# Stationary tiles of the 512-column products placed 16 words behind their streams modulo 128 (32 in the second feed-forward part) in place of 48

## The reference

```
def peer_ffn(xn, w_pq, sub_keys1, sub_keys2, expert_down, expert_up):
    def block(xb):
        qh = (xb @ w_pq).reshape(T, P_HEADS, 2, P_KEY_DIM).astype(jnp.float32)
        ...
        top_s, pos = lax.top_k(cand_s, P_TOPK)
        eidx = jnp.take_along_axis(cand_i, pos, axis=-1)
        g = jax.nn.softmax(top_s, axis=-1)
        u = expert_down[eidx]
        a = jax.nn.gelu(jnp.einsum('thkd,td->thk', u, xb), approximate=False)
        coef = (g * a.astype(jnp.float32)).astype(xb.dtype)
        return jnp.einsum('thk,thkd->td', coef, expert_up[eidx])

def conv_ffn(hn, w_up, conv_w, conv_b, w_down):
    u, v = jnp.split(hn @ w_up, 2, axis=-1)
    ...
    return (jax.nn.silu(uc) * v) @ w_down

def second_block(x, ...):
    h = x
    for layer in range(DEPTH_2):
        ...
        h = h + mix.astype(h.dtype)
        hn = rms_norm(h, ffn_norm_g[layer])
        h = h + conv_ffn(hn, ffn_w_up[layer], ffn_conv_w[layer], ffn_conv_b[layer], ffn_w_down[layer]).astype(h.dtype)
    return h
```

## Time and profile before

| what | value |
|---|---|
| runs, median (lowest to highest) | 1668.53 us (1667.17 to 1670.89) |
| span of the profiled execution | 1670.5 us |
| PE busy | 1652.9 us, 99% |
| PE's weight loads busy | 1542.5 us, 92% |
| DVE busy | 1237.3 us, 74% |
| ACT busy | 935.2 us, 56% |
| POOL busy | 242.8 us, 15% |
| DMA, mean over the span | 194 GB/s |

### The profile page before, as it was taken

How to read it: one execution, slowest core, us unless ns; L and a number is a source line. 1 busy time by engine, 2 the same in 40 slices (tenths; PEclk the granted TensorE clock), 3 DMA queues, 4 the chain that set the end, 5 groups by cost and what they waited for, 6 DMA issues and landing times.

```text
span 1670.5 us, 30280 instructions
## 1 busy us (share of the span) xinstructions
PE 1652.9 (99%) x12006; PEld 1542.5 (92%) x12006; DVE 1237.3 (74%) x1896; ACT 935.2 (56%) x1139; POOL 242.8 (15%) x333
## 2 busy tenths in 40 slices
PE   8999999999999999999999999999999999999999
PEld 8999999999999999988888888999999888899987
DVE  6875467999998666667676676887888565769974
ACT  7885565555546555545555454786545357565542
POOL 0000000004667676211010110000000000100000
PEclk9999999999999999999999999999999999999999
DMA  7445344776555555777777776533555544345553
GB/s 304 152 152 180 120 159 157 231 233 213 189 178 191 190 189 191 270 240 238 245 235 239 241 238 222 221 133 139 184 185 195 180 174 152 124 156 203 200 188 115
DMA packets 73804, 323.40 MB, mean 194 GB/s; under 512 B 8663, under 2 KB 9047, under 8 KB 55744
## 3 DMA queue, kind: packets, MB, share of 16 engines
q1 hardware_dynamic: 58736, 285.18, 50.1%
q0 software_dynamic: 5568, 19.38, 3.7%
q10 hardware_dynamic: 9360, 16.92, 2.7%
HBM read 303.62 MB, written 17.83 MB: 192 GB/s over the span
## 4 chain that ended last, share of the span: by engine, by line
PE 83%; DVE 12%; ACT 4%; issue 1%; DMA 0%; SPq 0%; ACTq 0%; DVEq 0%
PE bank L605 14%; PE bank L606 13%; PE bank L607 13%; PE bank L986 7%; PE bank L985 7%; PE bank L987 7%; PE bank L938 5%; PE bank L942 5%; PE bank L941 5%; DVE lo_u L2299 3%; PE bank L950 2%; DVE wlo L1914 2%; DVE oh L2310 1%; ACT whi L1350 1%; DVE pos L2196 1%
## 5 line engine op out<-in xcount | busy, mean ns | idle before, releaser
L1586 ACT ACTIVATE hi_u<-raw_u 128x1024 fp32r<-128x1024 f32 x256 | 271.8, 1062 | 279.6 <-PE bank L985 165.2
L1914 DVE TENSOR_TENSOR wlo<-raw,whi 128x2048 fp32r<-128x2048 f32 (+1 forms) x141 | 314.7, 2232 | 105.6 <-PE bank L605 83.3
L1350 ACT ACTIVATE whi<-raw 128x2048 fp32r<-128x2048 f32 x137 | 263.1, 1920 | 77.6 <-PE bank L605 74.7
L938 PE MATMUL bank<-xh,hi_u 128*128 128x256 f32 x1024 | 291.9, 285 | 1.5 <-DVE lo_u L2299 1.2
L2299 DVE TENSOR_TENSOR lo_u<-raw_u,hi_u 128x1024 fp32r<-128x1024 f32 x192 | 237.9, 1239 | 70.4 <-PE bank L938 62.4
L941 PE MATMUL bank<-xl,hi_u 128*128 128x256 f32 x1024 | 285.4, 279 | 0.0
L942 PE MATMUL bank<-xh,lo_u 128*128 128x256 f32 x1024 | 285.3, 279 | 0.0
L605 PE MATMUL bank<-nh,whi 128*128 128x256 f32 x904 | 253.4, 280 | 0.5 <-DVE wlo L1914 0.4
L607 PE MATMUL bank<-nh,wlo 128*128 128x256 f32 x904 | 251.9, 279 | 0.0
L606 PE MATMUL bank<-nl,whi 128*128 128x256 f32 x904 | 251.9, 279 | 0.0
L519 POOL TENSOR_SCALAR oh<-kept,sel_T 128x128 f32<-128x128 f32 x256 | 199.9, 797 | 249.3 <-ACT sel_T L1636 166.4
(11 more groups left out here) (417 smaller groups left out, 3358.7 us busy)
## 6 DMA issues: line engine op xcount, KB each, us to landing
raw<-in_weights SPq DMA_DIRECT2D x138, 1024.0 KB, 4.8
raw_u<-in_experts SPq DMA_DIRECT2D x256, 512.0 KB, 4.2
aside<-a_out ACTq DMA_DIRECT2D x64, 256.0 KB, 3.6
a_in<-aside POOLq DMA_DIRECT2D x64, 256.0 KB, 3.7
const<-in_const SPq DMA_DIRECT2D x1, 1409.0 KB, 9.0
const<-in_const POOLq DMA_DIRECT2D x1, 1409.0 KB, 6.4
h<-in_x SPq DMA_DIRECT2D x2, 512.0 KB, 5.1
raw<-in_weights SPq DMA_DIRECT2D x2, 512.0 KB, 7.6
```

Source lines behind the costliest of these rows:

```text
L938: mm = pe.matmul(out, w[0][:, kp], xh[:, k, :], start=(k == 0), stop=False)
L1350: a(A(whi[:, n % HIGH, :], raw[:, n % RAW, :], ACT.Copy), S("weights_hi"))
L1586: a(A(hi_u[:, u % HIGH_U, :], raw_u[:, u % RAW_U, :], ACT.Copy), S("unit_high"))
L1914: v(V.tensor_tensor(wlo[:, n % LOW, place], raw[:, n % RAW, place], whi[:, n % HIGH, place].bitcast(F32), ALU.subtract), S("weights_split" ...
```

## The change

The address of four groups of tiles changes. In the expert stage `lo_up` goes to the front of its area, at 0 modulo 128 as before. `chi`, `clo` follow it at 16 in place of 48, and `g_final` after them. In the feed-forward parts `gh0`, `gl0` go from 48 to 16 and `gh1`, `gl1` from 48 to 32. The assertion keeps the area within the words that `xh` and `xl` leave free by then. No instruction, wait, transfer or size changes, and on each of the five engines the instructions with their waits stand in the same order as before.

```
@@ -360,11 +360,13 @@
         crossing = Area(CROSSING_AT)
+        crossing.beside(HIGH_AT, 0)
+        lo_up = crossing("lo_up", UNIT, dt=F32R)
+        crossing.beside(HIGH_AT, 16)
         chi = crossing("chi", 2, 2, T, dt=F32R)
         clo = crossing("clo", 2, 2, T, dt=F32R)
         g_final = crossing("g_final", D)
-        crossing.beside(HIGH_AT, 0)
-        lo_up = crossing("lo_up", UNIT, dt=F32R)
+        assert crossing.at <= CROSSING_AT + 2 * KD * T + 128
@@ -404,7 +406,7 @@
         f5 = Area(ARENA2 + 128)
         gated_of = []
-        for layer_, by in ((0, 48), (1, 48)):
+        for layer_, by in ((0, 16), (1, 32)):
             halves = Area(ARENA2)
             halves.beside(HIGH_AT, by)
```

## The result

The changed kernel takes 1678.0 us in the median (1676.5 to 1680.5), the kernel before beside it 1668.0. The ratio is 1.0058, 95% interval 1.0045 to 1.0070, so 9.7 us slower (7.5 to 11.7). I forecast 1664.0 and a range up to 1673; both were wrong, and so was the sign. The span of its profiled execution is 1674.6 us.

What follows compares the result with a forecast made beforehand. TensorE, busy 1652.9 of 1670.5 us, was taken to bound the kernel; 2.2 ns x 2040 matmuls = 4.5 us saved, from the runs' median 1668.5 to 1664.0 us, range 1650 to 1673.

Steps and rivals of the forecast that it cites:

- the sign: Whole kernel: faster 0.53, same 0.30, slower 0.17.
- PE sets the end, one for one: Whole kernel: TensorE busy 1652.9 of 1670.5 us; matmul cost in the long stages goes into the end one for one.
- Moving `lo_up` and the new places cost nothing: Expert stage: `lo_up` moves to the front of its area, written and read as before, cost 0.
- The first pair keeps 680 ns: Start of the expert stage: the untouched first pair, at distance 0 and 226.7 ns a matmul, does not change its pace.
- The step that failed: Expert stage and down products: 512-column matmuls at 16 and 32 go from 228.9 to 226.7 ns, saving 4.5 us; 0.36.
- The upper bound: Range's upper end, 1673 us: the 512-column stretches lock in at 231.1 ns a matmul.
- The slow rival: 512-column products at 16 can fall into the slow pace, 231.1 ns, costing 4.5 us, 1673.0 us; chance 0.18.
- The price per load: 512-column stages: a cost per load, pace 660 or 673 ns a round; chance 0.24, half for each value.
- the lower end of the range, 1650: Whole kernel: the best per-load value, 1650 us.
- the readings 660 and 673: Expert stage, L985 to L985: 660 or 673 ns a round would show the load's price.
- The smaller period: Only distance modulo a smaller number counts; 32 gives no gain at 16, 1667.9 to 1668.5 us; no change had 0.22.
- The flips: 256-column up products: a changed phase can flip their pace, 1056 matmuls x 4.5 ns = 4.7 us either way for each.

Runs made afterwards that it cites:

- the first four experiments: Against the kernel before: new tile order at distance 48, 1.0008; distances 0, 64, 80, 0.9991; two distances in one stage, 1.0036; other distances for 256-column products, 1.0113.

## Why the prediction was wrong

- **PE sets the end, one for one: right.** 8.8 us more in the 512-column rounds is 8.8 us more span where the up products agree, give or take the 1.5 us by which untouched stages vary. No wait appeared; PE is busy in all 330 us of the stretch.
- **Moving `lo_up` and the new places cost nothing: right**, by the run with the new order at 48 (1444 against 1443 matmuls).
- **The first pair keeps 680 ns: right.** It is untouched and stays at 680, and distance 0 is the reason: the whole stage runs at 680 once it is placed there.
- **The step that failed: "I take distance 16, and 32 between 16 and 48 with it, to reach 226.7".** Measured are 233.3 and 232.4 ns a matmul, not 226.7. I had carried the quick pace of the 256-column products at 16 over to 512 columns, because 113.3 and 226.7 are the same per column. That equality said nothing of distance 16 at 512 columns. Nor was 32 "between" 16 and 48 in any way that helps: the pace is not smooth in the distance. So the term of the sum that I put at 2040 x 2.2 ns = 4.5 us saved was 8.8 us lost. Distance 0 shows how little carries over: best for one shape (226.7) and worst for the other (120).
- **The upper bound was too low.** I took the slow pace's 4.5 ns per load over 226.7, 231.1. The measured 233.3 lies outside, since that bound too came from 256 columns.
- **The slow rival named the right direction.** It made the time 1673.0 and had 0.18. In the changed kernel every group of rounds at 16 is at 700; it isn't one of two paces chosen by the entry, so it was right that 16 costs more than 48 at this shape, and wrong that an entry decides it. That load and stream disturb one another there was my reading, and isn't shown; what is shown is that the address alone moves the pace, 700 against 686.7 ns a round. Its sum with the measured 4.4 ns is 1776 x 4.4 + 264 x 3.5 = 8.7 us, and 1677 us; the runs' median is 1678.0.
- **The price per load (0.24) and the lower end of the range, 1650, with the readings 660 and 673:** they rest on an estimate of mine for what the columns take without a load, and no run shows that term. What the runs showed: no 512-column stretch was under 680 ns a round, even where two of its three tiles had a quarter of the columns and loaded in 108 ns in place of 188 (690.0 at distance 0).
- **The smaller period:** 32 is refuted (16 and 48 differ by 13 ns), but a period of 64 is there (0 and 64, 16 and 80, 32 and 96, 48 and 112 agree within 0.4 ns a round), where I had put 128. For the period of 32 I had counted that the two 16s of the 256-column products, behind and before the stream, can't be told apart. They can: before the stream it is 353 ns a round nearly throughout.
- **The address counts:** the same instructions with tiles at another address take 680 to 703 ns a round.
- **The flips** were right in kind and size (4.2 of the 5.4 us of span between two executions of one program), and blurred the comparison of single profiles as I had said. I should have drawn from it that the profile shown was one with a slow draw: its span lay 2.0 us over the median of the runs, and wherever both are recorded for one execution, the run's time is 1.8 us longer than its span, which makes it 3.8. The times show the draws as well: of the 21 of the kernel before that stand beside the first four experiments, 14 lie from 1666.0 to 1669.3 us and 7 from 1670.8 to 1673.3.

## What to carry to other kernels

In this kernel, in stages where TensorE was busy without a gap (330.00 of 330.00 us), the address of the stationary tile against its stream was worth 3% of each 512-column matmul (680 to 703 ns a round), without any instruction changing. Measure it for each shape by itself. Here it repeats after 64 words at 512 columns (680 ns a round at 0 and 64, 700 at 16 and 80), and the best places were 0 for 512 columns (680) and 16 for 256, the latter with two paces (340 and 353). Whether another kernel has the same values isn't shown. The pace read on one shape was no bound for the other: from 113.3 ns at 256 columns I took 226.7 for 512, and 233.3 was measured. And profile a kernel twice before two spans are compared: the first up product took 117.8 ns a matmul in one execution of the kernel before and 113.3 in another.

## What the runs showed of the hardware that I had not expected

- The pace against distance isn't smooth: 680 at 0, then 700 from 8 on, 703 at 24, 697 at 32, 700 at 40, 687 at 48, 700 at 56, 680 at 64. The two distances under 690, 0 and 48, are single points among steps of 8 words.
- Paces that persist: 113.3 or 117.8 ns a matmul through 90 us and more of a 256-column product, and not the same one in each execution of a program; at 512 columns and distance 48, 687 or 701 ns a round, it seems by the rounds that came before.
- A stationary tile of a quarter of the columns loads in 108 instead of 188 ns, and yet the round at distance 0, with two such tiles, grows from 680 to 690.
